# The gated delta scan of a fused forward pass: group tail and next prelude interleaved, new values by the inverse, rows in four DMAs

## The reference, cut to what matters

```
a_mat = I + (kb k^T) * decay * strict          # kb = k * beta, per chunk and head
sol   = triangular_solve(a_mat, [v * beta, kb * exp(G)])   # -> u, w
attn  = (q k^T) * decay;  qd = q * exp(G);  kt = k * exp(G_last - G)
for each chunk:
    v_new = u - w S
    o     = qd S + attn v_new
    S     = S * exp(G_last) + kt^T v_new
```

## Time and profile before

| | |
|---|---|
| median of 3 runs | 1698.09 us (1696.57 to 1701.2) |
| profiled execution, its own time | 1694.21 us |
| its span | 1692.4 us |
| mean granted TensorE clock | 0.969 |
| busy: PE, DVE, ACT, GpSimd | 94%, 64%, 47%, 21% |
| the scan's four groups with the meta output copy | 176.41 to 340.99 us of the span |

### The profile page before, as it was taken

The page is one execution under the profiler, slowest core; times in us unless marked ns, Lnnn a source line. Parts: engine busy times, 40 slices in busy tenths (PEclk is TensorE's granted clock), DMA queues, the critical chain, the costliest instruction groups (busy, mean ns, idle before and its releaser), DMA issues.

```text
span 1692.4 us, 33972 instructions
## 1 busy us (share of the span) xinstructions
PE 1593.9 (94%) x14107; PEld 1516.3 (90%) x14107; DVE 1084.5 (64%) x1544; ACT 803.4 (47%) x1190; POOL 347.8 (21%) x347
## 2 busy tenths in 40 slices
PE   6998888889999999999999999999999898899998
PEld 6896877879999999998899999999987698899998
DVE  6784555446488855665788657665563765666653
...
DMA packets 42429, 252.73 MB, mean 149 GB/s; under 512 B 5504, under 2 KB 7664, under 8 KB 20304
## 3 DMA queue, kind: packets, MB, share of 16 engines
...
...
## 4 chain that ended last, share of the span: by engine, by line
PE 74%; DVE 9%; issue 9%; ACT 6%; DMA 2%; POOL 0%; SPq 0%; ACTq 0%; DVEq 0%; POOLq 0%
PE bank L422 20%; PE bank L423 20%; PE bank L424 20%; PE bank L1234 3%; DVE w_lo L297 2%; ACT w_hi L294 2%; DVE rs L577 1%; DMA sq<-rows_scratch_q 1%; PE bank L440 1%; PE bank L624 1%; ACT work L2294 1%; DVE mix L583 1%; PE bank L441 1%; PE bank L442 1%; PE bank L1315 0%
## 5 line engine op out<-in xcount | busy, mean ns | idle before, releaser
L422 PE MATMUL bank<-work_r,w_hi 128*128 128x256 f32 (+2 forms) x3248 | 927.8, 286 | 23.9 <-DVE w_lo L297 14.7
L423 PE MATMUL bank<-work_r,w_hi 128*128 128x256 f32 (+2 forms) x3248 | 921.1, 284 | 0.0
L424 PE MATMUL bank<-work_r,w_lo 128*128 128x256 f32 (+2 forms) x3248 | 920.9, 284 | 0.0
L297 DVE TENSOR_TENSOR w_lo<-ring,w_hi 128x2048 fp32r<-128x2048 f32 (+2 forms) x233 | 497.2, 2135 | 330.0 <-ACT w_hi L294 330.0
L422 PEld LDWEIGHTS bank<-work_r,w_hi 128*128 128x128 f32 x3248 | 619.2, 191 | 34.4 <-DVE w_lo L297 17.9
L294 ACT ACTIVATE w_hi<-ring 128x2048 fp32r<-128x2048 f32 (+2 forms) x233 | 408.3, 1754 | 453.9 <-PE bank L424 453.6
L423 PEld LDWEIGHTS bank<-work_r,w_hi 128*128 128x128 f32 x3248 | 618.6, 190 | 0.3
L424 PEld LDWEIGHTS bank<-work_r,w_lo 128*128 128x128 f32 x3248 | 617.7, 190 | 0.0
L1474 POOL TENSOR_TENSOR work<-work 128x272 f32<-128x272 f32 (+1 forms) x44 | 92.6, 2105 | 136.1 <-ACT work L1436 136.1
L533 POOL TENSOR_TENSOR sq<-sq 128x256 f32<-128x256 f32 (+2 forms) x36 | 57.5, 1598 | 250.9 <-ACT sq L511 250.1
L1462 DVE SCALAR_TENSOR_TENSOR work<-work,params_sb 128x272 f32<-128x272 f32 (+1 forms) x176 | 99.3, 606 | 5.1 <-DVE work L1462 0.3
(11 more groups left out here) (440 smaller groups left out, 1765.3 us busy)
## 6 DMA issues: line engine op xcount, KB each, us to landing
...
```

What stands on the lines that cost most here:

```text
L297: eng.tensor_tensor(w_lo[:, slot, 0:size], raw_w, w_hi[:, slot, 0:size].bitcast(F32), ALU.subtract).then_inc(lo_done, 1)
L422: pe.matmul(out, w_hi[:, slot, at:at + P], hi, start=first, stop=False)
L423: pe.matmul(out, w_hi[:, slot, at:at + P], lo, start=False, stop=False)
L424: mm = pe.matmul(out, w_lo[:, slot, at:at + P], hi, start=False, stop=last)
```

## The change

- The solve keeps `XT`; `w` is no longer formed. New values are `XT^T (beta v - beta exp(G) (k S))`: PE multiplies keys by the state (`keys_on_state`, two products of 256 columns a chunk), DVE adds it to beta v (`values`, four operations `scalar_tensor_tensor` of 128 columns a chunk), PE applies the inverse once. `nkbe`, wT, its ACT copies and the products w S go.
- The prelude of group g + 1 is issued inside the tail of group g on every engine: `ahead_keys_pe`, `ahead_values_pe`, `ahead_scores_pe`, `ahead_x_pe` between the tail's products; A on DVE (`ahead_keys_dve`) before and behind the state update. Banks are reassigned for it; kn and qd are double-buffered.
- GpSimd takes over from DVE: the causal sum, kn, qn, A * level0 and I - that. The subtraction of G moves into the exponential's bias (four ACT operations of 128 columns a chunk in place of one of 512); its column is stored negated. The copy of v and the copy of the state go. The group's XT is cleared once, not in each group.
- Rows come in four DMAs (G, norm, beta, exp G; all but norm without the meta tokens), each issued by GpSimd as soon as its rows are read.
- attn and ktl are spread: chunk 2's at level 1, chunk 1's at levels 2 and 3, the decayed state at level 4.
- For group 0 the prelude is issued behind the meta chunk, with the memsets waiting for the meta outputs.

The diff, cut to its core:

```diff
-        kn = area(8704 + 4896, 2, T)
-        qd = area(8704 + 5440, 4, T)
-        vs = area(8704 + 6528, 4, T)
-        St = area(8704 + 7616, 4, P)
+        kn = [area(8704 + 4896, 2, T), area(6144, 2, T, of=spare)]
+        qd = [area(8704 + 5440, 4, T), area(8704 + 6528, 4, T)]
         St2 = area(8704 + 8128, 4, P)
...
-            fetch_gate_rows(pool, 0)
-            fetch_norm_rows(pool, 0)
+            for kind in ("G", "norm", "beta", "eG"):
+                fetch_rows(pool, kind, 0)
...
+            pool.wait_ge(*S.at("first_pe", "o"))
+            for c in CHUNKS:
+                inc(pool.memset(buf[c]["XT"][:, :, LOW], 0.0))
...
-            ahead_kn(dve, 0)
-            ahead_diff(dve, 0)
...
+        def kk_bank(c):
+            return bank(2, 3)[:, 256 * (c - 1):256 * c].rearrange("p (h n) -> p h n", n=P)
+        def token_bank(c):
+            return bank(1, 1) if c == 1 else bank(2, 3)
+        def score_bank(c):
+            return bank(1, 3) if c == 1 else bank(2, 1)
+        def state(g, c):
+            return St0[:, 4 * g:4 * g + 4, :] if c == 1 else St2
+        def fetch_rows(pool, kind, g):
+            lo, hi = ROWS[kind]
+            if kind == "norm":
+                dst = bc[:, lo:hi, :].rearrange("p (a b) t -> p a b t", b=2)
+                src = on_all(scratch, g * (2 * T), (8 * T, 2), (T, 2), (1, T))
+            else:
+                dst, src = bc[:, lo:hi, REST], on_all(scratch, (4 * lo + 4 * g) * T + META, (T, 4), (1, SEQ))
+            pool.dma_start(dst, src).then_inc(S.sem(f"{kind}_in"), 16)
+        def ahead_pool(pool, g):
+            inc = lambda ins, step=None: S.inc(ins, "ahead_pool", step)
+            own = lambda: S.own(pool, "ahead_pool", g)
+            arrived = lambda kind: pool.wait_ge(S.sem(f"{kind}_in"), 16 * (g + 1))
+            last = g == GROUPS - 1
+            def next_rows(kind):
+                if not last:
+                    own()
+                    fetch_rows(pool, kind, g + 1)
+            S.begin("ahead_pool")
+            arrived("G")
+            if g > 0:
+                pool.wait_ge(*S.at("scan_dve", "attn1", g - 1))
             for c in CHUNKS:
-                inc(pool.memset(buf[c]["XT"][:, :, LOW], 0.0), f"zero{c}")
-            inc(pool.tensor_tensor(by2(qd[:, :, META:T]), two(qn[:, :, META:T]), by2(bc[:, 12:16, META:T]), ALU.mult), "qd")
-            if not last:
-                pool.wait_ge(*S.at("scan_dve", "decayed", g))
-                pool.wait_ge(*S.at("scan_pool", "qd", g))
-                fetch_gate_rows(pool, g + 1)
-                fetch_norm_rows(pool, g + 1)
-                ahead_beta(pool, g + 1)
+                t0, n = TILES[c]
+                inc(pool.tensor_tensor(buf[c]["dec"], bc[:, 8:12, t0:t0 + n], over(cn("causal")[:, 0:P], 4), ALU.add), f"add{c}")
+            next_rows("G")
+            arrived("norm")
+            qk = work[:, 0:16 * T].rearrange("p (s g h t) -> p s g h t", s=2, h=2, t=T)
+            inc(pool.tensor_tensor(kn[g % 2][:, :, REST], qk[:, 1, g, :, REST], bc[:, 2:4, REST], ALU.mult), "kn")
+            arrived("beta")
+            for c in CHUNKS:
+                t0, n = TILES[c]
+                pool.wait_ge(*S.at("ahead_act", f"dec{c}", g))
+                inc(pool.tensor_tensor(buf[c]["decb"], buf[c]["dec"], bc[:, 4:8, t0:t0 + n], ALU.mult), f"decb{c}")
+                if c == 1:
+                    inc(pool.tensor_tensor(qn[:, :, REST], qk[:, 0, g, :, REST], bc[:, 0:2, REST], ALU.mult), "qn")
+            next_rows("norm")
+            next_rows("beta")
+            for c in CHUNKS:
+                pool.wait_ge(*S.at("ahead_dve", f"A{c}", g))
+                inc(pool.tensor_tensor(XT64[c], A64[c], over(level0, 4), ALU.mult))
+                own()
+                inc(pool.tensor_tensor(XT64[c], over(ident64, 4), XT64[c], ALU.subtract), f"XT{c}")
+            arrived("eG")
+            inc(pool.tensor_tensor(by2(qd[g % 2][:, :, REST]), two(qn[:, :, REST]), by2(bc[:, 12:16, REST]), ALU.mult), "qd")
+            last_token = TILES[1][0] + P - 1
+            inc(pool.tensor_copy(decay[:, g % 2, :], bc[:, 12:16, last_token]), "decay")
+            next_rows("eG")
...
+        def ahead_keys_dve(dve, g, c):
+            if c == 1:
+                S.begin("ahead_dve")
+                dve.wait_ge(*S.at("ahead_pe", "kk", g))
+            inc = lambda ins, step=None: S.inc(ins, "ahead_dve", step)
+            dve.wait_ge(*S.at("ahead_pool", f"decb{c}", g))
+            for out, rows, cols in ((A64[c][LOW], LOW, LOW), (A64[c][HIGH], HIGH, HIGH), (Aoff[c][LOW], LOW, HIGH)):
+                ins = inc(dve.tensor_tensor(by2(out), two(kk_bank(c)[rows, :, cols]), by2(buf[c]["decb"][rows, :, cols]), ALU.mult),
+                          f"A{c}" if cols != rows else None)
+        def ahead_exp(act, g, c):
+            if c == 1:
+                S.begin("ahead_act")
+            act.wait_ge(*S.at("ahead_pool", f"add{c}", g))
+            for h in range(4):
+                v = buf[c]["dec"][:, h, :]
+                ins = act.activation(v, v, ACT.Exp, bias=colv[:, c, 1, 4 * g + h:4 * g + h + 1])
+            S.inc(ins, "ahead_act", f"dec{c}")
+        def ahead_x_act(act, g, c):
+            act.wait_ge(*S.at("ahead_pe", f"X{c}", g))
+            S.inc(act.activation(X64[c], packed(bank(c, 0)), ACT.Copy), "ahead_act", f"X{c}")
+        def ahead_values_act(act, g, c):
+            act.wait_ge(*S.at("ahead_pe", f"vtok{c}", g))
+            for h in range(4):
+                ins = act.activation(buf[c]["vb"][:, h, :], tile4(token_bank(c))[:, h, :], ACT.Copy, scale=colv[:, c, 0, 4 * g + h:4 * g + h + 1])
+            S.inc(ins, "ahead_act", f"vb{c}")
+        H4 = range(4)
+        col = lambda h: slice(h * P, (h + 1) * P)
+        side = lambda h: slice(h * 64, (h + 1) * 64)
+        def by_halves(pe, out, left, right):
+            for h in H4:
+                for s in HALVES:
+                    mm = pe.matmul(out[s, side(h)], left[s, h, :], right[s, h, :], start=True, stop=True)
+            return mm
+        id4 = ident64.unsqueeze(1).broadcast_to([P, 4, 64])
+        def ahead_keys_pe(pe, g):
+            S.begin("ahead_pe")
+            pe.wait_ge(*S.at("ahead_pool", "kn", g))
+            if g > 0:
+                pe.wait_ge(*S.at("ahead_act", "vb2", g - 1))
+            for c in CHUNKS:
+                t0, n = TILES[c]
+                for h in range(2):
+                    k = kn[g % 2][:, h, t0:t0 + n]
+                    mm = pe.matmul(kk_bank(c)[:, h, :], k, k, start=True, stop=True)
+            S.inc(mm, "ahead_pe", "kk")
...
+        def ahead_values_pe(pe, g, c):
+            t0, n = TILES[c]
+            if c == 2:
+                pe.wait_ge(*S.at("ahead_dve", "A2", g))
+            elif g > 0:
+                pe.wait_ge(*S.at("scan_act", "vn1", g - 1))
+            for h in H4:
+                mm = pe.transpose(token_bank(c)[:, col(h)], qkv[:, 16 + 4 * g + h, t0:t0 + n], ident)
+            S.inc(mm, "ahead_pe", f"vtok{c}")
+        def ahead_scores_pe(pe, g, c):
+            t0, n = TILES[c]
+            pe.wait_ge(*S.at("ahead_pool", "qn", g))
+            if g > 0:
+                pe.wait_ge(*(S.at("scan_dve", "S", g - 1) if c == 1 else S.at("scan_act", "vn2", g - 1)))
+            for h in range(2):
+                k = kn[g % 2][:, h, t0:t0 + n]
+                pe.matmul(score_bank(c)[:, col(h)], k, qn[:, h, t0:t0 + n], start=True, stop=True)
+                mm = pe.transpose(score_bank(c)[:, col(2 + h)], k, ident)
+            S.inc(mm, "ahead_pe", f"kq{c}")
+        def ahead_x_pe(pe, g, c):
+            pe.wait_ge(*S.at("ahead_pool", f"XT{c}", g))
+            S.inc(by_halves(pe, bank(c, 0), XT64[c], id4), "ahead_pe", f"X{c}")
...
+            def decayed_state():
+                dve.wait_ge(*S.at("ahead_pool", "decay", g))
+                if g > 0:
+                    dve.wait_ge(*S.at("scan_pe", "o2", g - 1))
+                inc(dve.tensor_tensor(St2, state(g, 1), down(decay[:, g % 2, :], P), ALU.mult))
+            def values(c, source):
+                dve.wait_ge(*S.at("scan_pe", f"kS{c}", g))
+                dve.wait_ge(*S.at("ahead_act", f"vb{c}", g))
+                v = buf[c]["vb"]
+                for h in H4:
+                    inc(dve.scalar_tensor_tensor(out=v[:, h, :], in0=source[:, col(h)], scalar=colb[:, c, 4 * g + h:4 * g + h + 1], in1=v[:, h, :],
+                                                 op0=ALU.mult, op1=ALU.add), f"R{c}.{h}")
+            beside = {1: (lambda: attn(2), lambda: keys(2)), 2: (lambda: attn(1), nothing_more), 3: (lambda: keys(1), nothing_more),
+                      4: (decayed_state, nothing_more), 5: (nothing_more, nothing_more)}
...
+            values(1, bank(1, 3))
             for c in CHUNKS:
                 dve.wait_ge(*S.at("scan_pe", f"XX{c}.{TOP}", g))
                 inc(dve.tensor_scalar(buf[c]["XT"][LOW, :, HIGH], packed(bank(c, 2))[LOW], -1.0, None, ALU.mult), f"XT{c}.{TOP}")
```

(63 more changed lines are left out.)

215 lines of the change are left out of this document (53 added, 162 removed).

## The result

The changed kernel takes 1667.06 us (median; 1666.01 to 1673.47) where the kernel before takes 1698.59 us beside it: ratio 0.9842, 95% interval 0.9810 to 0.9874, or 26.8 us (21.4 to 32.3). Its profiled execution took 1667.9 us, its span 1666.1 us. The forecast was 1672 (1662 to 1685). A later series with the same changed kernel gave 0.9884 (0.9854 to 0.9915), 19.7 us; the mean of both is 23.2 us.

What follows compares the result with a forecast made beforehand. It took the scan to be a latency chain handed between PE, DVE and ACT, no engine full. Terms -22.4 - 2.0 - 4.1 + 8.0 - 4.9 = -25.4 us took 1698.1 to about 1672, range 1662 to 1685.

Steps and rivals of the forecast that it cites:

- Joints: Tail of a group plus next prelude, interleaved: 11.6 us instead of 19.07, -7.5 at each of three joints, -22.4.
- the walk: PE's queue followed from the end of level 6 through a joint, to see whether PE stays full; no late wait found.
- Levels: Levels 1 to 5 of each group, with lighter work beside and keys on state added: -0.5 a group, -2.0.
- Last tail: Tail of the last group, nothing to interleave: 8.5 us instead of 12.6 to the last ACT copy, -4.1.
- First prelude: Group 0's prelude, now exposed behind the meta scan with GpSimd in series: 14.4 us for 7.43, +8.0 with additions.
- Fetch gaps: PE's code waiting behind row DMAs in the groups: cost 7.9 us before, 3 after with smaller pieces, -4.9.
- (a): Rival: fetch gaps become the bound, four a group plus a half-clock stretch, 17 us; -11.4, 1687 us; chance 0.16.
- (b): Rival: GpSimd holds DVE after all, PSUM readers included, costing 18 us; -7.4, 1691 us; chance 0.07.
- (c): Rival: GpSimd sets the pace, about 41 us a group and a longer first prelude; about +15, 1713 us; chance 0.05.
- (d): Rival: interleaved order queues something late ahead of something urgent on PE at each joint; no gain, 1697 us; chance 0.03.

Runs made afterwards that it cites:

- e2: Kernel before, with groups 1 to 3 fetching their rows onto one partition instead of 128; 1687.29 us, ratio 0.9968.
- e4: Kernel before, with new values by the inverse applied to corrected values and no interleaving; 1689.84 us, ratio 0.9977.
- e1: Changed kernel, with each group's rows fetched in two DMAs again instead of four; 1668.96 us, ratio 0.9851.
- second run: The changed kernel itself run again, with nothing altered; 1674.89 us, ratio 0.9884.
- e5: Changed kernel, with group 0's GpSimd and ACT preparation run beside the meta scan, only memsets and XT waiting for meta outputs; 1660.75 us, ratio 0.9800.
- e9: Kernel before, with rows of groups 1 to 3 on one partition and new values by the inverse, not interleaved; 1680.82 us, ratio 0.9908.
- e7: Changed kernel, with DVE's decayed state made at level 2, beside GpSimd's causal sums, instead of level 4; 1671.84 us, ratio 0.9878.
- e6: Changed kernel, with group 0 prepared beside the meta scan and its row DMAs issued behind the first masked products; 1662.91 us, ratio 0.9819.

## Why the prediction was right, step by step

The time fell inside the range, 5 us under the forecast, and the mechanism was the likeliest one. As a difference, 25.4 us lies between the two series of the changed kernel, 26.8 and 19.7. By its terms:

- **Joints, -22.4.** 12.23 us each where the walk gave 11.6; PE waits for no other engine in them, so what was mis-sized is the units and the allowance of 0.3 us, not a wait. In the first joint scores and key transposes took 1.75 us for their 12 units (1.34), and the two batches of X 1.22 for 1.0; a batch of eight products took its 0.89 or up to 0.24 more. The old joint without gaps is e2's mean group, 38.68, less 19.86 of levels, 18.8. So -6.6 each, **-19.8**.
- **Levels, -2.0.** 19.24 us against the walk's 2.75 + 12.24 + 0.89 + 3.49 = 19.37: **-2.5**.
- **Last tail, -4.1.** 12.6 us became 9.6, not 8.5: **-3.0**. Mis-sized is above all the time from a batch of PE to the engine that reads it, taken at 1.0 us (1.2 for the last new values), that is the products alone. It took 1.17 to 1.24 us each of five times, 0.8 us together. The rest is the wait for XT, 0.4 where 0.3 was named, with DVE's corrected values ahead of XT and nothing to cover them (as in e4), and the first corrected value of chunk 2, 0.46 for 0.3. Timeline of the kernel after, first batches of the last tail:

```profile
306.62 0.97 PEld L1337 LDWEIGHTS bank<-mix,sq 128*128 128x128 f32 x8 [0.65 <-DVE sq L1255]
307.82 0.60 ACT L1288 ACTIVATE sq<-bank 128x512 f32<-128x512 f32 x1 [2.44 <-PE bank L1337]
308.47 0.97 PEld L1379 LDWEIGHTS bank<-sq,mix 128*128 128x128 f32 x8
309.67 0.69 DVE L1260 TENSOR_TENSOR work<-work,bank 128x512 f32<-128x512 f32 x1 [2.77 <-PE bank L1379]
```

- **First prelude, +8.0.** 17.26 us for 8.12, **+9.1**, and ahead of the scan's stretch 0.6 us more from DVE's XT0 to the meta output (41.71 for 41.15), where 0.5 was named: 9.7 in all. Mis-sized: a GpSimd operation of 256 columns at half of 512's, 0.63, where it takes 0.72; 0.30 us idle ahead of each DMA issue that waits for GpSimd's own result; and the lower clock until 190.3. GpSimd's chain ended 13.9 us after the meta output where 12.9 was summed, and the first Y product followed 2.7 us later, where 1.5 and 0.5 for the clock were named (e1, at full clock there, was 1.1 us faster over that end). In the second run it was 18.40. The term was right in its nature, and e5 shows it was avoidable.
- **Fetch gaps, -4.9.** They had cost 9.0 and one gap with 1.3 us stayed: **-7.7**, the largest miss of a term, to the good side. With rows of 0.5 MB no gap was longer than 1.4 us in any run, and in the kernel after the clock never fell inside a group. The 1.7 us that the prediction gave each stretch at the lower clock is too much for one in a prelude, where e9 lost 0.8 us at most up to the first Y, against e2.

Together -23.9, where the traced scan has -23.4. With the 0.6 us ahead of it the terms give -23.3 for the forecast's -25.4, and they missed by up to 3 us in both directions: joints, last tail and first prelude gave 5.4 us less than forecast, gaps and levels 3.3 more. The mechanism was right; that the sum came out as close as it did is in part luck.

The rivals: (a) is out, four gaps a group did not come; with two DMAs (e1) one a group came back. (b) is out: bank readers kept 0.42 beside GpSimd, and the corrected values of chunk 2 their 1.13 (216.49 in the kernel after, while GpSimd made XT). (c) is out for the groups (1.26 us for 512 columns, groups of 31.47 us set by PE), but GpSimd did set the pace for 13.9 us ahead of group 0 (to the end of XT, 188.49), at its normal rate, for want of cover. (d) is out: PE is full in the joints.

Of the Trainium skill's rule on the port (SBUF — State Buffer, "SBUF: two separate sides"), that whoever starts first has the shared pair for the whole instruction and the other fully blocks, the prediction used one side only. The trace of e7 agrees, and shows the other: 0.94 for 0.68 us on DVE, then 2.95 for 2.51 on GpSimd. A whole instruction is short here, so each side lost only the rest of one. The other rule of the Trainium skill, that elementwise work belongs on VectorE (GPSIMD Engine Reference, "Engine selection"), was the wrong question here: e5 left all of it on GpSimd and got back 8.0 us by moving it under other work. No run put these operations on DVE.

What stays open: some 4 us from run to run outside the scan, so that no time here can tell e6 from e5; and why e9's clock falls in every prelude where e2's mostly holds, though e2's PE waits there just as long.
